# Attention of an encoder layer in two stages: dilated heads by near keys and residue classes, grouped heads with stationary values, group norms in the output stage

## The reference, cut to what matters

```python
DILATED_PATTERNS = ((128, 1), (512, 4), (2048, 16))   # (window, dilation)
def mixer_dilated(q, k, v):
    for window, dil in DILATED_PATTERNS:   # |distance| <= window // 2 and a multiple of dil
        o, l = dilated_branch(q, k, v, window, dil)
        ...
    w = jax.nn.softmax(jnp.stack(lses, 0), axis=0)
    o = jnp.sum(w[..., None] * jnp.stack(outs, 0), axis=0)
...
def mixer_axial_gqa(q, k, v):              # every query sees all keys of its request
    s = jnp.einsum('bqkgd,bskd->bkgqs', qblk, k) * scale
    return jnp.einsum('bkgqs,bskd->bqkgd', jax.nn.softmax(s, axis=-1), v)
...
o = jnp.concatenate([rmsnorm(o_a, on_a_g), rmsnorm(o_b, on_b_g)], axis=-1)
x = x + g1 * jnp.dot(o, w_out)
h2 = rmsnorm(x, ln2_g) * (1 + sc2) + sh2
x = x + g2 * hier_moe(h2, ...)             # 4 groups of 8 experts, 2 experts of one group
```

## Time and profile before

| | |
|---|---|
| three runs | 1917.48 us median, 1915.33 to 1920.99 |
| profiled execution: span | 1923.3 us |
| TensorE busy, of the span | 1674.4 us, 87% |
| VectorE, ScalarE, GpSimd busy | 1146.6, 922.6, 296.4 us |
| TensorE from 396.4 to 446.4 (keys) | 24.59 of 50.00 us, granted clock 0.57 |
| from 446.4 to 989.4 (attention) | 529.69 of 543.00 us, clock 0.97 |
| from 989.4 to 1018.2 (to the first output product) | 1.95 of 28.80 us, clock 0.51 |
| from 1018.2 to 1180.0 (output stage) | 153.89 of 161.80 us, clock 0.94 |
| from 1180.0 to the end | 592.14 of 743.00 us, DMA busy 0.88 |

### The profile page before, as it was taken

How to read it: one execution, slowest core, us unless ns; L and a number is a source line. 1 busy time by engine, 2 the same in 40 slices (tenths; PEclk the granted TensorE clock), 3 DMA queues, 4 the chain that set the end, 5 groups by cost and what they waited for, 6 DMA issues and landing times. The chain is left out here.

```text
span 1923.3 us, 27791 instructions
## 1 busy us (share of the span) xinstructions
PE 1674.4 (87%) x9314; PEld 1376.1 (72%) x9314; DVE 1146.6 (60%) x1557; ACT 922.6 (48%) x1337; POOL 296.4 (15%) x329
## 2 busy tenths in 40 slices
PE   9959999959999999999958994399999999999900
PEld 1118888848989989999956883288888888888700
DVE  2323444444545545555544444598988988988758
ACT  1111221235545545555542221278878878878622
POOL 0100111101211211021210000101101101100077
PEclk9979999968999999999978996699999999999955
DMA  9951222146000000000024236389999999999564
GB/s 374 396 187 55 74 74 91 41 179 256 12 34 28 34 12 29 28 26 20 12 103 153 98 132 231 108 293 405 409 399 411 403 407 402 406 406 397 224 236 168
DMA packets 113973, 372.79 MB, mean 194 GB/s; under 512 B 15164, under 2 KB 19260, under 8 KB 113892
## 3 DMA queue, kind: packets, MB, share of 16 engines
q1 hardware_dynamic: 101188, 327.47, 44.5%
q0 software_dynamic: 8096, 27.42, 4.1%
q10 hardware_dynamic: 4608, 16.78, 2.2%
HBM read 317.30 MB, written 54.33 MB: 193 GB/s over the span
## 5 line engine op out<-in xcount | busy, mean ns | idle before, releaser
L1603 DVE TENSOR_TENSOR exp_w_lo<-ring_raw,exp_w_hi 128x1024 fp32r<-128x1024 f32 x376 | 437.9, 1220 | 46.8 <-ACT exp_w_hi L1547 42.4
L1547 ACT CAST exp_w_hi<-ring_raw 128x1024 fp32r<-128x1024 f32 x376 | 368.1, 1051 | 52.5 <-PEq L90 30.4
L937 PE MATMUL att_op<-kv_v,att_pT 128*128 128x64 f32 x2176 | 268.0, 276 | 0.8 <-DVE att_o L856 0.7
L937 PEld LDWEIGHTS att_op<-kv_v,att_pT 128*128 128x128 f32 x2176 | 258.2, 194 | 1.3 <-DVE att_o L856 1.1
L787 ACT COPY att_pT<-att_tp 128x512 f32<-128x512 f32 (+1 forms) x160 | 83.3, 521 | 249.7 <-PE att_tp L922 249.0
L911 PE MATMUL att_sc<-kv_kT,att_qT 128*128 128x512 f32 (+1 forms) x576 | 174.4, 422 | 5.4 <-issue 3.4
L781 ACT ACTIVATE att_prob<-att_s,att_neg_max 128x1024 f32<-128x1024 f32 (+1 forms) x160 | 164.1, 1026 | 7.5 <-DVE att_neg_max L840 7.4
L922 PE MATMUL att_tp<-att_ident_f,att_prob 128*128 128x128 f32 x1088 | 150.9, 279 | 9.1 <-DVE att_pT L846 8.6
L840 DVE CUSTOM_DVE_ANT_0 att_s<-att_sc,att_counts 128x1024 f32<-128x1024 f32 (+1 forms) x80 | 85.0, 1063 | 120.7 <-PE att_sc L911 111.2
L922 PEld LDWEIGHTS att_tp<-att_ident_f,att_prob 128*128 128x128 f32 x1088 | 131.2, 145 | 30.4 <-issue 14.0
L840 DVE CUSTOM_DVE_ANT_0 att_s<-att_sc,att_zero 128x1024 f32<-128x1024 f32 (+1 forms) x80 | 85.1, 1064 | 112.0 <-PE att_sc L911 109.6
(11 more groups left out here) (240 smaller groups left out, 2936.4 us busy)
## 6 DMA issues: line engine op xcount, KB each, us to landing
ring_raw<-in_w SPq DMA_DIRECT2D x376, 512.0 KB, 6.0
mod_ring<-in_w_ada SPq DMA_DIRECT2D x48, 512.0 KB, 6.0
y<-exp_y ACTq DMA_DIRECT2D x32, 512.0 KB, 7.0
y<-att_zeros SPq DMA_DIRECT2D x1, 9728.0 KB, 32.3
mod_wraw<-in_w_in SPq DMA_DIRECT2D x16, 576.0 KB, 6.6
mod_ring<-in_w_adaf SPq DMA_DIRECT2D x16, 512.0 KB, 6.8
prj_x<-in_x_all SPq DMA_DIRECT2D x10, 512.0 KB, 3.7
q<-prj_stage SPq DMA_DIRECT2D x20, 256.0 KB, 2.0
```

Of the source, the lines that this page charges most:

```text
L937: mm = pe.matmul(op[:, h * HD:(h + 1) * HD], pT[:, j % 2, half, i, :], v_sb[:, v0 + half * c + i, col:col + HD], start=(half == 0 and i == ...
L1547: act.copy(w_hi[:, to, :], src).then_inc(hi_done, 1)
L1603: dve.tensor_tensor(w_lo[:, to, :], raw_at(e, c)[0], w_hi[:, to, :].bitcast(F32), ALU.subtract).then_inc(lo_done, 1)
```

## The change

The values of the dilated heads are stored with a 65th column of ones, so that a product with the values yields the sum of the probabilities as well. `stage_keys` is gone, and `stage_attention` is two stages.

`stage_dilated` walks over the 8 dilated heads, and in a head over 9 steps, one for each prompt tile and one for the sample. A step has two blocks of 128 queries by 256 keys: x = 0 is a tile of queries and the keys around it; x = 1 is 128 queries of one residue class modulo 4 (stride 4 in `qT`) and the 256 keys of that class. The splits and transposes of the next head's keys and queries (9 groups of two to four transposes) stand between the steps. A score block is now two products: the high and low parts of q (128 rows, `qT`) against the high part of k, which `kT` holds twice, and the high part of q against the low part of k (64 rows, `kL`). The two partial results of a query, its sum and its maximum go to DRAM as `near` and `far`, 66 numbers each.

`stage_grouped` walks over units of a query tile and a key head with four heads each. The values, high and low part side by side, are stationary, and the turned probabilities of four heads (512 columns, high and low parts) stream: four f32r products for a quarter of the keys in a step. A unit's result is transposed and its two halves are added by four f32 products with a folded identity, two units later. The joining of `near` and `far` runs beside it on GpSimd, VectorE and ScalarE.

The mean squares, `pow` and the scaling of both groups are now in `stage_output`, for tile t+1 at the head of `body(t)`, and the transposes of t+1 wait for them. The diff, cut to its core:

```diff
+                        act.copy(values[:, :, 0:HD], pp[n][:].rearrange("p (h d) -> p h d", d=HD)).then_inc(copied[n], 1)
+                    else:
+                        act.copy(stage[:, lo:hi], pp[n][:, 0:hi - lo]).then_inc(copied[n], 1)
...
+        def turns_at(i):
+            return range((3 * i + 1) // 2, (3 * i + 4) // 2) if i < 6 else ()
...
+                for g in range(2):
+                    sp.wait_ge(o_kept, 3 * h + 2 + g)
+                    sp.dma_start(far_dram[g * 512:(g + 1) * 512, h, :].rearrange("(p c) d -> p c d", c=4),
+                                 ob[:, b, 4 * g:4 * g + 4, 1, :]).then_inc(stored[b], 16)
+                sp.dma_start(near_dram[0:S0, h, :].rearrange("(t p) d -> p t d", p=P), ob[:, b, 0:NT0, 0, :]).then_inc(stored[b], 16)
+                sp.dma_start(near_dram[S0:T, h, :].rearrange("(t p) d -> p t d", p=P), ob[:, b, NT0, :, :]).then_inc(stored[b], 16)
...
+                for x in range(2):
+                    if i == NT0:
+                        table = 5 + x
+                    elif x == 0:
+                        table = 0 if i == 0 else 2 if i == NT0 - 1 else 1
+                    else:
+                        table = 3 + i // 4
+                    step = dve.tensor_tensor_reduce(s[:, n % 2, x, :], sc[n % 2][:, x * WIN:(x + 1) * WIN], counts[:, table, :], -SCALE, 3e38,
+                                                    ALU.add, ALU.min, ob[:, h % 2, i, x, HD + 1:BW])
+                step.then_inc(masked, 1)
...
+                for x in range(2):
+                    if i == NT0:
+                        rows, keys = slice(S0 + x * P, S0 + (x + 1) * P), slice(SAMPLE, SAMPLE + WIN)
...
+                        rows, keys = slice(i * P, (i + 1) * P), slice(i * P, i * P + WIN)
...
+                        g, c = divmod(i, 4)
+                        rows, keys = slice(g * 512 + c, (g + 1) * 512, 4), slice(PAD + c, PAD + S0, 4)
+                    out = sc[n % 2][:, x * WIN:(x + 1) * WIN]
+                    pe.matmul(out, qT[:, b, rows], kT[:, b, keys], start=True, stop=False)
+                    mm = pe.matmul(out, qT[0:HD, b, rows], kL[:, b, keys], start=False, stop=True)
+                mm.then_inc(scores_ready, 1)
...
+                for j in range(4):
+                    mm = pe.transpose(tp[n % 2][:, j * P:(j + 1) * P], prob[:, n % 2, j // 2, (j % 2) * P:(j % 2 + 1) * P], ident_f[:])
...
+                    c = (2 * (n % 3) + x) * VW
+                    for j in range(2):
+                        if i == NT0:
+                            v = v_sam[:, j, h, :]
+                        elif x == 0:
+                            v = v_near[:, i + j, h, :]
+                        else:
+                            v = v_far[:, 4 * j + i % 4, h, :]
+                        mm = pe.matmul(op[g % 2][:, c:c + VW], pT[:, n % 2, 2 * x + j, :], v, start=(j == 0), stop=(j == 1))
...
+            for i in range(NGR):
+                turn(0, i)
+            scores(0)
+            scores(1)
+            for n in range(LAST):
+                h, i = divmod(n, STEPS)
+                if n + 2 < LAST:
+                    scores(n + 2)
+                p_transposes(n)
+                if h + 1 < NHA:
+                    for j in turns_at(i):
+                        turn(h + 1, j)
+                else:
+                    for j in turns_b_at(i):
+                        turn_b(j)
+                if n:
+                    values(n - 1)
...
+            def keep_oT(u):
...
+                dve.tensor_copy(oT[:, u % 2].rearrange("p h t -> p (h t)"), ot[:]).then_inc(oT_kept, 1)
...
+            for n in range(LAST):
+                u, hh = STEPS[n]
+                if n + 2 < LAST:
+                    mask(n + 2)
+                if FIRST_OF[u] == n and u >= 2:
+                    keep_oT(u - 2)
+                keep_lo(n)
+                for kind, w in shared_at(n):
+                    if kind == "fold":
+                        take_o(w)
...
+                    for c in range(0, S0, HALF):
+                        out = sc[n % 2][:, c:c + HALF]
+                        pe.matmul(out, qT[u % 2][:, hh, :], kT[:, kv, c:c + HALF], start=True, stop=False)
+                        mm = pe.matmul(out, qT[u % 2][0:HD, hh, :], kL[:, kv, c:c + HALF], start=False, stop=True)
...
+                    for p in (p_hi, p_lo):
+                        mm = pe.matmul(ot[:], v2[:, c0 + c, kv].rearrange("p a d -> p (a d)"),
+                                       p[:, u % 2, c].rearrange("p h t -> p (h t)"),
+                                       start=(c == 0 and p is p_hi), stop=(c == n_ch - 1 and p is p_lo))
...
+                    pe.wait_ge(oT_kept, u + 1)
+                    for j in range(G):
+                        mm = pe.matmul(gp[:, j * HD:(j + 1) * HD], oT[:, u % 2, j, :], fold[:], start=True, stop=True)
...
+            for n in range(LAST):
+                u, hh = STEPS[n]
+                if n + 2 < LAST:
+                    scores(n + 2)
+                p_transposes(n)
+                for kind, w in shared_at(n):
+                    use(kind, w)
+                if u:
+                    if hh is None:
+                        values(u - 1, 0, 1)
+                    else:
+                        values(u - 1, hh, G)
...
+            def group_scale(t, b):
+                pool.wait_ge(mso_ready, 2 * t + 2)
+                pool.tensor_tensor(rso[:, b, :], mso[:, b, :], neghalf[:], ALU.pow).then_inc(rso_ready, 1)
...
+            def scale_o(t, b):
+                act.wait_ge(rso_ready, t + 1)
+                for g in range(2):
+                    cols = slice(g * WA, (g + 1) * WA)
+                    step = act.activation(o[:, b, cols], o[:, b, cols], ACT.Copy, scale=rso[:, b, g:g + 1])
+                step.then_inc(o_scaled, 1)
...
+                    scale_o(t + 1, 1 - b)
                     split_hi(t + 1, 1 - b)
...
+            def group_squares(t, b, u):
+                dve.wait_ge(o_loaded[b], (u + 1) * 16)
...
+                    dve.tensor_tensor_reduce(osq[:], o[:, b, cols], o[:, b, cols], 1.0 / WA, EPS, ALU.mult, ALU.add,
+                                             mso[:, b, g:g + 1]).then_inc(mso_ready, 1)
...
-                pe.wait_ge(o_loaded[b], (u + 1) * 16)
+                pe.wait_ge(o_scaled, t + 1)
...
+    key, row = np.arange(WIN)[None, :], np.arange(P)[:, None]
+    near, far, every = [(1, 64)], [(1, 64), (4, 256)], [(1, 64), (4, 256), (16, 1024)]
+    tables = [counted(key - 64 - row, near, ok) for ok in (key >= 64, key >= 0, key < WIN - 64)]
+    tables += [counted(key - P * g - row, far) for g in range(2)]
+    tables += [counted(key - P * g - row, every) for g in range(2)]
+    return np.concatenate(tables, axis=1).astype(np.float32)
```

More of the change, by code:

```diff
@@ L566, in _ @@
+            for b in range(2):
+                sp.wait_ge(stored[b], 64 * (NHA // 2))
+            sp.wait_ge(zeros_stored, 16)
         @block.gpsimd
@@ L724, in _, with load_q, load_branches @@
-            tiles(sp, body)
-            for g in range(2):
-                sp.wait_ge(stored[g], 16 * (NT + 1))
-            sp.wait_ge(zeros_stored, 16)
+            def load_q(t):
+                sp.dma_start(q[:, t % 2, :], q_dram[t * P:(t + 1) * P, WA:2 * WA]).then_inc(q_loaded[t % 2], 16)
+            def load_branches(t):
+                rows = slice(t * P, (t + 1) * P)
+                sp.dma_start(near[:, t % 2], near_dram[rows]).then_inc(parts_loaded[t % 2], 16)
+                if t < NT0:
+                    sp.dma_start(far[:, t % 2], far_dram[rows]).then_inc(parts_loaded[t % 2], 16)
@@ L729, in _ @@
+            for b in range(2):
+                sp.wait_ge(stored[b], 16 * (NT // 2))
+                sp.wait_ge(joined[b], 16 * (NT // 2))
         @block.gpsimd
@@ new lines, in keep_hi, with keep_q @@
+            def keep_hi(n):
+                u, hh = STEPS[n]
+                for half in range(2):
+                    act.wait_ge(tp_ready[half], n + 1)
+                    if hh in (0, None) and u >= 2 and half == 0:
+                        act.wait_ge(pv_ready, u - 1)
+                    act.copy(*halves(p_hi, u, hh, half)).then_inc(hi_kept[half], 1)
+            def keep_q(n):
+                for kind, u in shared_at(n):
+                    if kind != "fold":
+                        act.wait_ge(used, TURN[kind, u] + 1)
+                        act.copy(qT[u % 2][:].rearrange("p h t -> p (h t)"), gp[:]).then_inc(qT_kept, 1)
```

861 lines of the change are left out of this document (535 added, 326 removed).

## The result

The changed kernel takes 2060.28 us in the median of four runs (2049.65 to 2060.61), against 1916.46 us before: a ratio of 1.0731 (95% interval 1.0703 to 1.0758), 7% slower. The profiled execution has a span of 2058.4 us, 135.1 more than before. The forecast was 1871 us.

A forecast was written before the change was run, and what follows sets the result against it. TensorE was taken as the bound, at nearly full clock. The rebuilt stretch gave 92 us less and the output stage 45 more, so 47 less than before: 1871 us, own range 1848 to 1893, whole range 1798 to 1920.

The forecast's parts named there:

- A dilated step: Dilated stage: a step of 2.27 us on TensorE, a head 23.9, eight heads 191 us.
- The price of a change: Score products: each switch between 128 and 64 rows costs TensorE 0.10 us, with bounds of 0 and 0.16.
- The rival that went by this rule: Both attention stages: each row change drains TensorE, 0.16 for 0.10 us, 35 us more, 1906 us; chance 0.18.
- The half-clock rival: Dilated stage: TensorE gaps from hand-overs between engines keep the clock at 0.50, doubling 191 us, 2062 us; chance 0.10.
- Start: Last projection product to first transposes of probabilities: 21.9 us in place of 50.0, 28 us less.
- Boundary between the stages: Between dilated and grouped stage: last results copied and stored, grouped stage set up, 12 us.
- Grouped stage: Grouped attention: 16 units of 15.7 us are 251, sample units 20, the end about 8: 279 us.
- To the first output product: Attention's end to first output product: 25.7 us for 28.85, as mean square, pow and scaling are gone.
- The output stage: Output stage: transposes wait 3.4 us a tile for the norm, plus 2.2 of clock; eight tiles 45 us more.
- The wait before the fold: Grouped stage: each unit's fold waits about 1.2 us for VectorE's copy, which stands behind a mask.
- the forecast's first rival: Both attention stages: the 64-row products cost nothing extra, 58 us less, 1813 us; chance 0.22.

The follow-up runs named there:

- e14: Changed kernel with all dilated score products on 128 rows and an overwritten product of 64 rows and 16 columns ahead of each block: 1937.45 us.
- e1: Changed kernel with 128 rows in the dilated stage's second score product, the lower half of kL being zeros: 1880.55 us.
- e2: Changed kernel with 60 products of 512 columns ahead of the dilated stage's first scores, to begin at full clock: 2066.08 us in one run.
- e13: Changed kernel with the 64-row product first in block x = 1 (two row changes a step) and 60 products of 512 columns ahead: 1916.18 us.
- e15: Changed kernel with both dilated score products on 64 rows (q's low by k's high part left out) and 60 products of 512 columns ahead: 2012.86 us.
- e3: Changed kernel with 128 rows in the grouped stage's second score product, zeros in the lower half of kL: 1995.61 us.
- e9: Changed kernel with the output stage's load of o issued two tiles ahead and the squares taken where VectorE waits: 2022.08 us.
- e5: Changed kernel with 128 rows in the second score product of both the dilated and the grouped stage: 1823.41 us.
- e6: Changed kernel with the 64-row product first in the dilated stage's block x = 1, two row changes a step for four: 1906.18 to 1991.10 us.
- e10: Changed kernel with VectorE's copy for the fold (gqa_oT) ahead of the mask of the step after next: 2034.97 us.
- e4: Changed kernel with the output stage's squares of tile t+2 put ahead of the hidden row of tile t: 2076.50 us.

## Why the prediction was wrong

**The step that failed** is "A dilated step", its sum of 191 us, and in it the clock. It added full-clock spacings for a stage with TensorE busy throughout and took for granted that busy meant full clock. It was 353 us: 100% busy at 0.50. That is 162 of the 189 us by which the forecast missed. A head takes 45.0 us (553.62 to 598.58); in e14, with four changes a step as well, it takes 28.2 at full clock. By this, as an estimate, 8 x 16.8 = 134 of the 162 are the clock, and the rest is what the changes cost above 0.10 and the stride, which the sum left out. The runs put in the place of that step: the mixture of 128 and 64 rows in this stage's score products keeps TensorE at 1.2 GHz (e1 against the changed kernel: 180 us), and both the number of changes and the amount of work on 64 rows count (e2, e13, e15).

**The price of a change**, 0.10 with bounds of 0 and 0.16, was too low: 0.17 on average at full clock by the starts, 0.18 by e3, 0.68 for a step's four where the forecast had 0.40. The Trainium skill, "TensorEngine Tiling (Array Packing)", Key Properties, says that a change of the tiling mode drains TensorE. The trace agrees in that each change costs time; what the engine does in it, no run shows. The rival that went by this rule had the price right, at 0.16, and missed by 154 us all the same, for the clock.

**The half-clock rival** gave 2062 for the whole stage, and 2060 was measured. That agreement is luck. The rival doubled 191 to 382, where 353 was measured, and its reason isn't the one: it wanted gaps from hand-overs between engines, and the profile shows no wait of TensorE in this stage. Its chance of 0.10 was argued down by the absence of gaps, and the clock was down without them.

The other terms mostly held. Start: 24.7 us from the last projection product (395.82) to the first transposes of probabilities (420.47), forecast 21.9. Boundary between the stages: 16.3, forecast 12; 7.7 of it is a wait for VectorE's `gqa_fold`. Grouped stage: 298.6, forecast 279, at 16.5 a unit for 15.7, which the price of the changes explains; the rest is its first steps at half clock. To the first output product 25.3 (1088.6 to 1113.94), forecast 25.7. The output stage, from its first to its last product of `out_yp`, takes 184.9 for 148.3 before: 36.6 more, forecast 45. Its wait was 3.3 per tile for the forecast 3.4, so the clock was priced too high there; e9 shows that the wait is on the path. The wait before the fold was 1.0, forecast 1.2.

Without the row changes the forecast's first rival said 1813; e5, which has none, took 1823. The structure of the change was worth about what the sum said, but errors cancel in it. The dilated stage took 183 us in e5, where 162 are left of the forecast without its changes, for the stride and for some half clock at its start. The grouped stage took 241 for 250, and the output stage gave back 38 for 45. One layout choice turned the result over.

What stays open: how much of the clock's fall is from the changes and how much from the work on 64 rows; what decides when the clock rises in e6, e10 and e14; and why the grouped stage, with the same alternation, ran at 0.99. Its products have 512 columns and no stride, and no run varies either. In e1 and e5 the stride is there at a clock of 1.00, so alone it doesn't hold the clock down.

## What to carry to other kernels

Halving the rows of a contraction saved TensorE nothing: products of 256 columns on 64 rows start 0.12 us apart in a row (e15, 429.93 and 430.05), as those on 128 do. Each switch of row count cost 0.17 us on average, so padding to 128 rows with zeros was the faster form (1823 against 2060). Where a stage is made of short products, read the granted clock beside the busy share, and forecast at both levels: a busy share of 100% says only that the profile shows no wait. When a small computation is moved into a later loop, move its load ahead with it (e9 against e4).

## What the runs showed of the hardware that was not expected

- The clock stayed at 0.50 for 353 us with no idle time in TensorE's records, and was 1.00 in the same stage with 128-row products and more arithmetic (e1). The busy column counts a product with its pause: a product of 512 columns behind a change is recorded with 0.50 us, in place of 0.39.
- The same instructions ran at either level. With two changes a step the clock was 0.50 for 200 us in one profiled run from a start at half clock, and 1.00 throughout from a start at full clock (e6, e13); the twelve runs of e6 spread over 85 us.
- A change between 128 and 64 rows costs 0.20 us at full clock within a row of them (0.43 in place of 0.23 at 512 columns, 0.31 in place of 0.12 at 256), the first of a row about 0.1, and within a row about 0.3 at half clock (0.51 to 0.53 in place of the 0.24 between a 128-row product and what follows it in e14, at 500.40 and 500.64).
- Score products whose queries and keys are both taken with a stride of 4 cost more at full clock: 0.31 and 0.24 us to the next start, in place of 0.11 and 0.13 (e1, all on 128 rows).
